# First weight stage, first up-projection tile and gating stage of a hybrid decoder layer: order of the work changed

## The reference

```python
xn = rmsnorm(h, g_mix); u = xn @ w_in              # 1024 x 6144, ten groups of columns
# hgrn2 and retention branches, merged:
h = h + mixed @ w_out
xn = rmsnorm(h, g_ffn)
a, g = split(xn @ w_up, 2)                         # each 2816 wide
ac = conv_b + sum(padded[:, j:j + l] * conv_w[j] for j in range(3))   # causal, width 3
h = h + (gelu(ac) * g) @ w_down
gate = sigmoid(rmsnorm(h, g_ple) @ w_ple_gate)
h = h + gate * (p @ w_ple)
y = rmsnorm(h, g_final)
```

## Time and profile before

| | us |
|---|---|
| median of 3 runs | 927.93 (927.81 to 927.96) |
| the profiled execution, its own time | 926.42 |
| its span (first to last instruction) | 924.3 |
| PE busy in it | 905.6 |
| DVE busy | 524.8 |
| ACT busy | 391.2 |
| POOL busy | 234.5 |

### The profile page before, as it was taken

The page is one execution under the profiler, slowest core; times in us unless marked ns, Lnnn a source line. Parts: engine busy times, 40 slices in busy tenths (PEclk is TensorE's granted clock), DMA queues, the critical chain, the costliest instruction groups (busy, mean ns, idle before and its releaser), DMA issues. The chain is left out here.

```text
span 924.3 us, 21150 instructions
## 1 busy us (share of the span) xinstructions
PE 905.6 (98%) x8046; PEld 892.6 (97%) x8046; DVE 524.8 (57%) x633; ACT 391.2 (42%) x523; POOL 234.5 (25%) x289
## 2 busy tenths in 40 slices
PE   6999999999999999999999999999999999999996
PEld 5999999999999999999999999999999999999995
DVE  6432278788754566665576666666666433434654
ACT  7323446556454565323354444444443222223433
POOL 0007077787111100004621111111111122212341
PEclk9999999999999999999999999999999999999998
DMA  6333533233254443633323333333333333332212
GB/s 226 92 93 92 183 93 89 71 91 101 59 137 136 136 119 109 201 118 100 91 69 93 91 91 91 91 91 91 91 91 108 94 94 94 94 91 82 80 45 93
DMA packets 176473, 94.74 MB, mean 103 GB/s; under 512 B 17889, under 2 KB 174961, under 8 KB 176017
## 3 DMA queue, kind: packets, MB, share of 16 engines
q1 hardware_dynamic: 149698, 80.61, 29.3%
q10 hardware_dynamic: 26736, 13.60, 5.4%
HBM read 86.25 MB, written 8.03 MB: 102 GB/s over the span
## 5 line engine op out<-in xcount | busy, mean ns | idle before, releaser
L1190 DVE TENSOR_TENSOR wlo<-raw,whi 128x1024 fp32r<-128x1024 f32 (+2 forms) x132 | 195.2, 1479 | 173.8 <-ACT whi L846 173.8
L846 ACT ACTIVATE whi<-raw 128x1024 fp32r<-128x1024 f32 (+2 forms) x132 | 146.6, 1111 | 337.7 <-PE acc L494 332.6
L494 PE MATMUL acc<-xah,whi 128*128 128x260 f32 x896 | 185.6, 288 | 0.0
L494 PE MATMUL acc<-xah,wlo 128*128 128x260 f32 x896 | 180.3, 283 | 0.0
L494 PE MATMUL acc<-xal,whi 128*128 128x260 f32 x896 | 179.8, 282 | 0.0
L494 PE MATMUL acc<-xbh,whi 128*128 128x260 f32 x816 | 165.3, 284 | 0.8 <-issue 0.8
L494 PE MATMUL acc<-xbh,wlo 128*128 128x260 f32 x816 | 164.4, 283 | 0.0
L494 PE MATMUL acc<-xbl,whi 128*128 128x260 f32 x816 | 164.2, 283 | 0.0
L494 PEld LDWEIGHTS acc<-xah,whi 128*128 128x128 f32 x896 | 138.1, 189 | 1.8
L494 PEld LDWEIGHTS acc<-xal,whi 128*128 128x128 f32 x896 | 137.9, 188 | 0.0
L494 PEld LDWEIGHTS acc<-xah,wlo 128*128 128x128 f32 x896 | 137.9, 188 | 0.0
(11 more groups left out here) (291 smaller groups left out, 1175.3 us busy)
## 6 DMA issues: line engine op xcount, KB each, us to landing
raw<-in_w_in SPq DMA_DIRECT2D x96, 256.0 KB, 3.1
raw<-in_w_up SPq DMA_DIRECT2D x88, 256.0 KB, 3.1
raw<-in_w_down SPq DMA_DIRECT2D x16, 384.0 KB, 3.3
raw<-in_w_down SPq DMA_DIRECT2D x16, 320.0 KB, 3.8
raw<-in_w_out SPq DMA_DIRECT2D x16, 256.0 KB, 2.9
raw<-in_w_ple_gate SPq DMA_DIRECT2D x8, 512.0 KB, 3.7
x_transposed<-xstg SPq DMA_DIRECT2D x1, 2080.0 KB, 7.3
hT<-x_transposed ACTq DMA_DIRECT2D x1, 2080.0 KB, 8.4
```

The lines of the kernel that those rows point to most:

```text
L494: mm = pe.matmul(sums[:, b, 0:HT], wt[slot][:, w], xx[:, c, b * HT:(b + 1) * HT], start=first and i == 0 and q == 0, stop=last and i == n ...
L846: act.activation(whi[k % 2][:, 0:n], raw[k % 2][:, 0:n], ACT.Copy).then_inc(hi_ready, 1)
L1190: dve.tensor_tensor(wlo[k % 2][:, 0:n], raw[k % 2][:, 0:n], whi[k % 2][:, 0:n].bitcast(fp), SUB).then_inc(lo_ready, 1)
```

## The change

In the first stage, PE gets `keep_busy(n)`: n products of two constant matrices into `acc[0]`, whose result nobody reads, 17 in all. `vectors` moves ahead of the third block of tokens, and DVE's first multiplication of `xsm` ahead of the third and fourth scaling. A sixth bank (`mb`) takes chunk 5, so only chunks 6 and 7 wait for a bank, and their transposes move into the first product, behind its second chunk. DVE's first `wlo` is cut into two halves, the second behind the `xal` of chunk 1; PE waits for the first half only, and for the second at chunk 4.

In F, ACT copies the first tile's sums unscaled into `ab` and so frees `acc[0]`; DVE takes the reciprocal in two halves, with the `wlo` of the third tile between them, and scales `ab` afterwards. ACT's `whi` of the fourth tile moves behind its first convolution step. The first round stands ahead of the loop, which has nine rounds left.

In H, `mean_square(1)` moves behind chunk 6; a sigmoid of a constant follows the root on ACT; ACT's `whi` of the third tile moves ahead of the first `sgg`, DVE's `wlo` of it ahead of the first L1564; `y_tile` comes in pairs behind products 2, 4 and 6.

The diff, cut to its core:

```diff
@@ x_bank
-            return (ob[:], acc[1][:, 0, :], acc[1][:, 1, :], lvb[:, 0, :], lvb[:, 1, :])[j % 5]
+            return (ob[:], acc[1][:, 0, :], acc[1][:, 1, :], lvb[:, 0, :], lvb[:, 1, :], mb[:])[j % 6]
@@ tensor
+            def keep_busy(n):
+
+                for _ in range(n):
+                    pe.matmul(acc[0][:, 0, 0:128], ones128[:], ones1024[:], start=True, stop=True)
+
+            pe.wait_ge(set_up, 2)
+            keep_busy(5)
             pe.wait_ge(ident_loaded, 16)
...
+            keep_busy(1)
...
                 raw_rows(n)
+                if n in (1, 2):
+                    keep_busy(1)
...
             for i in range(NCH):
+                if i == 2:
+                    vectors()
                 if i == NCH - 1:
-                    vectors()
+                    keep_busy(2)
                 pe.wait_ge(x_norm, i + 1)
                 for j in range(5):
                     if i == 0 and j >= 3:
+                        if j == 4:
+                            keep_busy(2)
                         pe.wait_ge(lv_free[j - 3], 2)
...
-            for j in range(5, DC):
-                pe.wait_ge(xa_lo, j - 5 + 2)
-                for i in range(NCH):
-                    mm = x_columns(i, j)
-                mm.then_inc(x_tile, 1)
+            pe.wait_ge(misc_free, 3)
+            for i in range(NCH):
+                mm = x_columns(i, 5)
+            mm.then_inc(x_tile, 1)
+            keep_busy(5)
+
+            def late_columns():
+
+                for j in range(6, DC):
+                    pe.wait_ge(xa_lo, j - 6 + 2)
+                    for i in range(NCH):
+                        mm = x_columns(i, j)
+                    mm.then_inc(x_tile, 1)
...
-                    product("A", k, it, k % 2, k, C8, 0, xah, xal,
-                            chunk_wait=(lambda c: pe.wait_ge(xa_lo, c + 2)) if it == 0 and k == 0 else None)
+                    if it == 0 and k == 0:
+                        def columns_split(c):
+                            if c == 4:
+                                pe.wait_ge(lo_ready, 3)
+                            pe.wait_ge(xa_lo, c + 2)
+
+                        pe.wait_ge(hi_ready, 1)
+                        pe.wait_ge(lo_half, 1)
+                        product("A", 0, 0, 0, 0, range(2), 0, xah, xal, last=False, wait_unit=False,
+                                chunk_wait=columns_split)
+                        late_columns()
+                        product("A", 0, 0, 0, 0, range(2, DC), 2, xah, xal, first=False, wait_unit=False,
+                                chunk_wait=columns_split)
+                    else:
+                        product("A", k, it, k % 2, k, C8, 0, xah, xal)
...
-                        if c == 6:
+                        if c == 7:
                             mean_square(1)
...
-                if j == 1:
+                if j == 2:
                     pe.wait_ge(acc_free[0], tidx("H", 2, 0, 8) + 1)
-                if j:
+                if j in (2, 4, 6):
+                    y_tile(j - 2, j - 2)
                     y_tile(j - 1, j - 1)
+                if j == DC - 1:
+                    y_tile(6, 6)
@@ scalar
-            def ffn(it, nxt=None):
+            def ffn(it, nxt=None, first=False):
                 for k in range(4):
                     done("F", k, it)
-                    ahead("F", k, it, nxt)
+                    if not (first and k == 1):
+                        ahead("F", k, it, nxt)
+                    if first and k == 0:
+
+                        act.activation(two(ab[0][:, 2:TT + 2]), ps2(0), ACT.Copy).then_inc(acc_free[0], 1)
+                        act.wait_ge(f_first, 1)
...
+                        if first and k == 0:
+                            done("F", 1, 0)
+                            ahead("F", 1, 0)
...
-            with act.Fori(0, 10) as it:
+            ffn(0, first=True)
+            with act.Fori(1, 10) as it:
...
+            act.activation(ssx[:, 6:7], eps[:], ACT.Sigmoid)
...
+                if j == 0:
+
+                    done("H", 1, 0, 8)
+                    ahead("H", 0, 0)
...
-                if j < DC - 2:
+                if 0 < j < DC - 2:
                     ahead("H", k, it)
...
@@ vector
-            token_scale(2, 3)
-            token_scale(3, 4)
             dve.wait_ge(misc_full, 2)
             dve.tensor_tensor(xsm[:], mb[:, 0:NS].unsqueeze(1).broadcast_to([128, DC, NS]), xstg[:, :, NT:TT],
                               MUL).then_inc(misc_free, 1)
+            token_scale(2, 3)
+            token_scale(3, 4)
...
-            lo("A", 0, 0)
+
+            def first_lo(h):
+                cols = slice(h * 512, h * 512 + 512)
+                dve.wait_ge(hi_ready, 1)
+                dve.tensor_tensor(wlo[0][:, cols], raw[0][:, cols], whi[0][:, cols].bitcast(fp), SUB)\
+                    .then_inc(lo_ready if h else lo_half, 1)
+
+            first_lo(0)
...
+                if j == 1:
+                    first_lo(1)
...
-            inverse_rms(0)
-
-            def ffn(it, nxt=None):
+            dve.wait_ge(lv_free[0], L_F // 2 + 1)
+            dve.reciprocal(rstd[:, 0:HT], rstd[:, 0:HT])
...
-                        dve.tensor_tensor(two(a[:, 2:TT + 2]), ps2(k), two(rstd[:]), MUL).then_inc(acc_free[0], 1)
-                        ahead("F", k, it, nxt)
+                        if first and k == 0:
+                            ahead("F", 0, 0)
+                            dve.wait_ge(lv_free[1], L_F // 2 + 1)
+                            step(dve.reciprocal(rstd[:, HT:TT], rstd[:, HT:TT]))
+                            dve.wait_ge(acc_free[0], tidx("F", 0, 0) + 1)
+                            dve.tensor_tensor(a[:, 2:TT + 2], a[:, 2:TT + 2], rstd[:], MUL).then_inc(f_first, 1)
+                            dve.wait_ge(f_first, 1)
...
                 done("H", 2 * k + 1, it, 8)
+                if j == 0:
+                    ahead("H", 0, 0)
...
-                if j < DC - 2:
+                if 0 < j < DC - 2:
                     ahead("H", k, it)
```

More of the change, by code:

```diff
@@ L260, in hybrid_layer @@
         lo_ready = sem("lo_ready")
+        lo_half = sem("lo_half")
         part_done = sem("part_done")
@@ L327, in hybrid_layer @@
         st_loaded = sem("st_loaded")
+        f_first = sem("f_first")
         c_first = sem("c_first")
@@ L1158, in _ @@
                 act.activation(yT[:, j, :], hT[:, j, :], ACT.Copy, scale=vc[:, 32 + j:33 + j]).then_inc(y_ready, 1)
-                if j % 2:
-                    y_copy(j - 1, j - 1)
+                if j in (2, 4, 6):
+                    y_copy(j - 2, j - 2)
+                if j == DC - 1:
+                    y_copy(6, 6)
             act.wait_ge(misc_full, M_G + 1)
@@ L1509, in ffn @@
                         a = ab[k // 2]
-                        dve.tensor_tensor(two(a[:, 2:TT + 2]), ps2(k), two(rstd[:]), MUL).then_inc(acc_free[0], 1)
-                        ahead("F", k, it, nxt)
+                        if first and k == 0:
[5 more added lines that the diff above has]
+                            dve.wait_ge(f_first, 1)
+                        else:
+                            dve.tensor_tensor(two(a[:, 2:TT + 2]), ps2(k), two(rstd[:]), MUL).then_inc(acc_free[0], 1)
+                            ahead("F", k, it, nxt)
                         dve.wait_ge(c_first, it * 2 + (k // 2 + 1))
@@ L1524, in ffn @@
                         dve.tensor_tensor(acl[:, j, :], gg[:], ach[:, j, :].bitcast(fp), SUB).then_inc(ac_lo, 1)
-            with dve.Fori(0, 10) as it:
-                step.loop(it, 4)
+            ffn(0, first=True)
+            with dve.Fori(1, 10) as it:
+                step.loop(it - 1, 4)
                 ffn(it)
-            step.end(10)
+            step.end(9)
             ffn(10, "G")
@@ L1718, in _ @@
             step.end(2)
+            pool.wait_ge(f_first, 1)
             with pool.Fori(0, 11) as it:
```

## The result

| | before | after |
|---|---|---|
| median | 927.87 (926.5 to 927.96, 4 runs) | 921.43 (921.26 to 922.2, 4 runs) |
| ratio | | 0.9936, 95% interval 0.9923 to 0.9948 |
| profiled execution, own time | 926.42 | 921.26 |
| its span | 924.3 | 919.5 |

The change gives 6.4 us. The forecast had the direction right and was too cautious. The two profiled spans differ by 924.3 - 919.5 = 4.8 us, which is the sum that the prediction made. So what was wrong is in the other 1.6, between the profiled execution and the median.

The account below looks back on a forecast made before the run. PE, busy 905.6 us, was taken as the bound, so only its idle or slow stretches pay: 2.4 (first stage) + 0.9 (F) + 1.5 (H) = 4.8 us, median 927.93 to 923.1; range 922.3 to 925.3.

Parts of the forecast that it names:

- 22.1 for the second product: First stage: the second product starts on PE at 22.1 us instead of 24.50.
- first product 15.1: First stage: PE can start chunk 0 of the first product at 15.1 us; before, it started at 18.17.
- F 0.9: First tile of F: PE's gap of 0.96 us ahead of the third tile goes, called 0.9 us gained.
- H 1.47: H: PE's gaps ahead of `mean_square(1)` and the first `y_tile` go, 0.68 + 0.79 = 1.47 us gained.
- it lies 1.5 under the median: Last step: profiled 926.42 becomes 921.6; as it lies 1.5 under the median, the median becomes 923.1.
- The first stage's term: First stage: the gain is how much sooner the second product starts, 24.50 - 22.1 = 2.4 us.
- A: First stage: the clock still falls to half under the first product; 1.7 to 2.2 us lost, 924.8 to 925.3; 17%.
- B: F: the chain to the fourth tile outlasts PE's next tile, `wlo` waiting for POOL's L1727; 924.5; 12%.
- C: First stage: gains and convolution weights haven't landed when PE wants them at about 11; 0.8 us lost, 923.9; 8%.
- D: First products: the clock stays at half long after the gap, over 13.4 us, making the kernel slower, 929.8; 2%.
- E: F or H: the edits give half of their worth or less by an unseen wait; 924.3; 6%.
- The rule on the clock gate: First stage: by this rule only constant products would hold the clock, making A likelier; the prediction found the trace disagreeing.

Follow-up runs that it names:

- e11: The changed kernel with four more constant products on PE between the sums of H's first squares and the wait for the last one; median 921.55.
- e10: The kernel before, unchanged, run again for its trace; profiled execution 927.39, median 927.09 (8 runs).
- e3: The changed kernel without its 17 constant products; median 921.86, ratio 0.9947.
- e7: The kernel before with the edits of the first stage and H, F as before; median 923.05, ratio 0.9951.
- e8: The changed kernel, run once more beside the others on one chip; median 921.6, ratio 0.9937.
- e2: The kernel before with all edits of the first stage, F and H as before; median 924.76, ratio 0.9975.
- e4: The kernel before with the edits of H alone; median 926.69, ratio 0.9995.
- e5: The kernel before with the edits of F alone; median 927.54, ratio 0.9995.
- e6: The kernel before with the edits of the first stage and F, H as before; median 923.1, ratio 0.9954.
- e9: The kernel before with only the vectors' transposes and DVE's first multiplication of `xsm` moved sooner; median 926.4, ratio 0.9988.

## Why the prediction was wrong

**The sum was right, and for its reasons.** Forecast 22.1 for the second product, measured 22.13; first product 15.1, measured 15.04; F 0.9, measured 1.03; H 1.47, measured 1.37 to 1.47; in all 4.8, and the spans differ by 4.8. The end is 0.1 longer, the middle 0.18 better than summed, and the clock record has no 0.50 under the first product. Some pieces of it were cheaper than worked out. ACT's first `whi` started at 12.05 instead of 12.36 because its load landed sooner, and the product still waited until 15.04 for the constant products ahead of it: they, not `xal`, ended last (`xal` of chunk 0 is written at 14.80). They started at 14.01 where 13.5 had been put down. That 22.13 meets 22.1 so closely is luck in part: in the six traces with all edits of the first stage the second product starts between 22.13 and 22.64, latest where the first `whi` had to wait longest for its load (e11: 12.84). The half `wlo` took 0.69, not 0.61.

**What failed** is the last step: "it lies 1.5 under the median, so the median of 927.93 becomes 923.1". That carries the 1.5 us over to the changed kernel as if they were in every execution of both. They are in the first stage, the very piece that the change rebuilds. The first stage's term, 24.50 - 22.1 = 2.4, is right for the execution of 926.42 and too small for a median one: 25.49 - 22.13 = 3.4. From e10's execution to after's, piece by piece: first stage 3.36, middle 2.53, end -0.2, outside the span 0.43, together 6.13, which is 927.39 - 921.26. Of the 1.5 us this opening accounts for 1.0; the other 0.5 lie between e10's 927.39 and the first session's 927.93, and before wasn't traced in an execution that long.

**A second part is smaller and was not thought of.** The time outside the span is 0.3 to 0.4 us shorter in after, e3, e7, e8 and e11, and not in e2, e4, e5 or e6; this holds in every execution (1.7 to 1.9 against 2.1 to 2.3), not only in the traced ones. It comes with the first stage and H together. Why is open; nothing in the span shows it.

**The rivals.** A (the clock falls under the first product) is what before does in the one execution near its median that was traced, and the changed kernel in none of its traces. B didn't come: the fourth tile's `wlo` is written at 478.30, 10.5 us behind the root, where 11.2 were worked out; and PE wants it 5.58 + 5.76 = 11.3 behind: 0.9 us of margin and not 0.1. DVE's scaling started at once behind the second half (0.23 had been put down for a wait), and from ACT's convolution step to the gate's read-out it went 0.2 faster. DVE's `wlo` (477.08, 1.22 us) had started first and POOL's L1806 took 1.84 instead of 1.31, as the Trainium skill, "SBUF — State Buffer", SBUF: two separate sides, would have it: whichever of the two starts first has the port for its whole instruction. C: the vectors were there by 11.71. D: nothing of it. E is false in the middle, but the end has a cost of its kind: e4 and e5 show how up to 1.2 us of a gain can be hidden by a fall of the clock under the last sums.

**The rule on the clock gate.** The Trainium skill, "TensorE: Matmul & The Clock Gate", Part 4, says that the full clock doesn't engage for transposes in the engine's transpose mode. Two more traces speak against it: in e3, which has no constant products, PE has done little but transposes when their distance goes from 0.21 to 0.11 us at about 13.8; in e10 the same happens between 12.9 and 13.6. With the constants it comes sooner than in most traces without (after's transposes are 0.11 apart from 10.2 on), but they are not needed for it. The kernel issues them with `pe.transpose`, and each leaves one record where a float32 product of two constants leaves two; still the records call them MATMUL and don't name the mode. So what is refuted is the rule as I used it, for this kernel's float32 transposes.

**Range.** It was 922.3 to 925.3, with 0.8 of room downwards for PE starting chunk 0 sooner. No part of it was for the profiled execution being a cheap one of before's. Median and profiled execution differed by 1.5, and the low end should have reached 923.1 - 1.5 = 921.6 for the case that all of it lies in a piece that the change removes. The rest down to 921.43 is in the time outside the span.

## What to carry to other kernels

When the profiled execution's own time differs from the median, don't shift the result by the difference. Ask first in which stage executions can differ (the opening, where loads land and the clock comes up, is the first suspect) and whether the change rebuilds that stage; if it does, work out the term a second time for a slow opening, and let the range hold both. And where several small edits are tried alone, compare pieces of the trace between fixed instructions beside the medians: here medians gave F 0.2 us and the trace 1.03, because the opening and the end of the kernel move by as much from execution to execution.

## What the runs showed of the hardware

- The record of the granted clock says 1.00 ahead of its first change even where PE is at half clock. In e10, transposes are 0.21 us apart up to 12.85 and 0.11 from 13.64 on, both at a recorded 1.00; in the first profile of before they are 0.11 apart from 8.3 on.
- The stretch at half clock behind the gap in the first stage is equally long wherever it comes, 3.4 us, worked out from the granted clock in windows of 0.2: 15.1 to 18.5, 16.6 to 20.0 (e10), 15.5 to 18.9 (e9), 15.7 to 19.1 (e4), 18.4 to 21.8 (e5). It costs half of the work that PE has under it, and least where it begins while PE stands still anyway, as in the earlier trace rows (2.81 us busy of 3.30).
- At the end of the kernel the clock falls again. Whether that comes ahead of the last sums or behind them is worth up to 1.2 us. What sets the moment is open.
